# First tile's output and query projections as a three-pass float32r split, fed by six slots of whole weight rows

## The reference, cut to what matters

```python
h  = h + mixed @ w_out                        # (tokens, 2048) @ (2048, 2048), float32
x  = rmsnorm(h, norm2_g)
qq = x @ peer_wq                              # (tokens, 2048) @ (2048, 2048)
s1, s2 = per head: qq halves @ k1.T, qq halves @ k2.T
...                                           # top 16 of each, top 16 of their sums -> 128 experts a token
out = sum over the 128 experts e: g * gelu(x . U[e]) * V[e]
```

## Time and profile before

| | |
|---|---|
| median of 3 runs | 2587.0 us (2580.58 to 2588.91) |
| the profiled execution: its own time | 2590.78 us |
| the profiled execution: its span | 2588.2 us |
| TensorE matmul busy | 2221.9 us (86% of the span) |
| VectorE busy | 1452.6 us (56%) |
| ScalarE busy | 399.5 us (15%) |
| DMA | 845.85 MB, mean 327 GB/s |

### The profile page before, as it was taken

One profiled execution on the slowest core, in us unless ns is written; L12 is line 12 of the kernel. 1 busy time (PEld: TensorE's weight loads), 2 busy tenths in 40 slices (PEclk: granted clock), 3 DMA queues, 4 the chain that ended last, 5 costly groups with the idle time before them and its releaser, 6 DMA issues.

```text
span 2588.2 us, 20434 instructions
## 1 busy us (share of the span) xinstructions
PE 2221.9 (86%) x7522; PEld 1221.3 (47%) x7522; DVE 1452.6 (56%) x2649; ACT 399.5 (15%) x846; POOL 380.8 (15%) x363
## 2 busy tenths in 40 slices
PE   6999999887999899997999997777777877777776
PEld 6999999655654444443444443233232322222221
DVE  4433333677300366568544557887888855555554
ACT  4223222323101101002000011111111100000000
POOL 0000000001000111212122121222222221222221
PEclk9999999876999899999999999999999999999999
DMA  5544444312668999999999999999999999999997
GB/s 180 183 137 138 155 131 130 114 53 66 212 243 286 352 426 392 407 425 387 414 425 401 414 407 422 415 411 401 421 408 412 410 429 428 428 428 428 428 429 298
DMA packets 159899, 845.85 MB, mean 327 GB/s; under 512 B 9814, under 2 KB 97682, under 8 KB 117162
## 3 DMA queue, kind: packets, MB, share of 16 engines
q0 software_dynamic: 46080, 671.11, 61.6%
q1 hardware_dynamic: 113722, 173.45, 19.9%
HBM read 834.31 MB, written 10.21 MB: 326 GB/s over the span
## 4 chain that ended last, share of the span: by engine, by line
PE 55%; DMA 29%; DVE 10%; issue 4%; ACT 1%; SPq 0%; POOL 0%; DVEq 0%; POOLq 0%; ACTq 0%
DMA rows_in<-in_peer_uv,expert 28%; PE bank L250 20%; PE bank L276 8%; PE bank L1038 5%; PE bank L1039 5%; PE bank L1037 5%; PE bank L263 4%; DVE rows_in L552 3%; PE bank L1214 1%; PE bank L1204 1%; DVE diag L527 1%; PE bank L1022 1%; PE bank L1132 1%; PE bank L1191 1%; PE bank L1120 1%
## 5 line engine op out<-in xcount | busy, mean ns | idle before, releaser
L250 PE MATMUL bank<-rows_in,diag 128*128 128x512 f32 (+1 forms) x2560 | 1188.5, 612 | 269.2 <-DVE diag L527 268.9
L552 DVE CUSTOM_DVE_ANT_0 rows_in<-rows_in,x2n 128x2048 f32<-128x2048 f32 x320 | 733.6, 2292 | 529.1 <-DMA rows_in<-in_peer_uv,expert 528.9
L250 PEld LDWEIGHTS bank<-rows_in,diag 128*128 128x128 f32 (+1 forms) x2560 | 452.9, 183 | 986.4 <-issue 546.5
L458 POOL DMA_INDIRECT rows_in<-in_peer_uv,expert x320 | 365.8, 1143 | 1489.5 <-PE bank L250 1304.7
L360 ACT ACTIVATE dots<-dots 128x1 f32<-128x1 f32 x320 | 64.9, 203 | 1515.9 <-DVE dots L552 1515.9
L1037 PE MATMUL bank<-xnh,wh 128*128 128x336 f32 (+2 forms) x928 | 293.1, 316 | 4.7 <-DVE wl L1452 4.7
L1038 PE MATMUL bank<-xnl,wh 128*128 128x336 f32 (+2 forms) x928 | 291.4, 314 | 0.0
L1039 PE MATMUL bank<-xnh,wl 128*128 128x336 f32 (+2 forms) x928 | 291.2, 314 | 0.0
L1452 DVE TENSOR_TENSOR wl<-wring,wh 128x2048 fp32r<-128x2048 f32 (+1 forms) x58 | 132.1, 2279 | 230.0 <-ACT wh L1272 230.0
L1037 PEld LDWEIGHTS bank<-xnh,wh 128*128 128x128 f32 (+1 forms) x928 | 174.6, 188 | 6.7 <-issue 5.4
L1038 PEld LDWEIGHTS bank<-xnl,wh 128*128 128x128 f32 (+1 forms) x928 | 174.6, 188 | 1.3
(11 more groups left out here) (291 smaller groups left out, 1355.3 us busy)
## 6 DMA issues: line engine op xcount, KB each, us to landing
wring<-in_w_in SPq DMA_DIRECT2D x28, 2048.0 KB, 8.3
wk<-in_w_out SPq DMA_DIRECT2D x64, 512.0 KB, 7.9
wk<-in_peer_wq SPq DMA_DIRECT2D x64, 512.0 KB, 8.4
kT<-in_keys_t SPq DMA_DIRECT2D x16, 512.0 KB, 5.3
vpage<-in_cache_v SPq DMA_DIRECT2D x16, 512.0 KB, 4.9
rows_in<-in_peer_uv,expert POOLq DMA_INDIRECT x320, 12.5
C<-in_state_C SPq DMA_DIRECT2D x4, 1024.0 KB, 6.0
out_C_sample<-C SPq DMA_DIRECT2D x4, 1024.0 KB, 4.4
```

What stands on the lines that cost most here:

```text
L250: mm = pe.matmul(accs[t][d][0:w, :], diag[r % ND][:, 0:w], rows_in[r % NG][:, D + 512 * d:D + 512 * d + 512], start=False, stop=(j == ROUN ...
L458: nc.gpsimd.indirect_dma_start(out=rows_in[r % NG][:], out_offset=None, in_=UV_DR, in_offset=bass.IndirectOffsetOnAxis(ap=ids[:, j:j + 1], ...
L552: nc.vector.tensor_tensor_reduce(u, u, x2n[t][:], 1.0, 0.0, ALU.mult, ALU.add, dots[t % 2][:, j:j + 1]).then_inc(S["dot_done"], 1)
```

## The change

For tile 0 the products with `w_out` and `peer_wq` are done by the three-pass split. The stationary operand is kept as `lh` and `ll` (high and low; from `mixA`, and then from the transposed banks of the norm). Weights come as whole rows of 128 x 2048 floats (1 MB) into six slots `wf`; ScalarE writes the high part to one of four slots `wfh` (`weight_high`), VectorE writes the low part over the row itself (`wfl`, `weight_low`). A row is requested once the row six before it has been used. The tail of tiles 1 and 2 keeps its half rows, but its first six wait until tile 0's last whole row has been used, and so do `h1[1]`, `h1[2]` and `gf`, which stand ahead of them. The diff, with allocations of semaphores and removed lines of the old half-row order left out:

```diff
-NG, ND, NW = 4, 4, 6
+NG, ND, NW, NF, NH = 4, 4, 6, 6, 4
...
+    def full_read(eng, n):
+        part, k = n // KC, n % KC
+        if k == KC - 1:
+            take(eng, (("wo", "wq")[part], 0, 3))
+        else:
+            eng.wait_ge(S["wk_used"], (KC - 1) * part + k + 1)
     def tail_sync(sp, out):
...
+        def full_rows(w, part, rows_=range(KC)):
+            for k in rows_:
+                n = KC * part + k
+                if n >= NF:
+                    full_read(sp, n - NF)
+                sp.dma_start(wf[n % NF][:], w[P * k:P * k + P, :]).then_inc(wf_in[n % NF], 16)
+        def weight_rows(w, part):
+            for row in range(2 * KC):
+                r = 2 * KC * (part - 2) + row
+                k, f = row % KC, row // KC
+                if r < NW:
+                    full_read(sp, 2 * KC - 1)
...
         sp.wait_ge(S["iqz_done"], 1)
-        weight_rows(a["w_out"][0], 0, range(NW))
+        full_rows(a["w_out"][0], 0, range(3))
...
-        weight_rows(a["w_out"][0], 0, range(NW, KC))
         evacuated(sp, ("sT2",))
+        full_rows(a["w_out"][0], 0, range(3, KC // 2))
         sp.dma_start(h1[0][:], xp[0:P]).then_inc(S["xr_in"], 16)
-        weight_rows(a["w_out"][0], 0, range(KC, 2 * KC))
+        full_rows(a["w_out"][0], 0, range(KC // 2, KC))
         broadcast(g2, a["norm2_g"][0], "g2_in")
-        weight_rows(a["peer_wq"][0], 1, range(KC))
+        full_rows(a["peer_wq"][0], 1, range(KC // 2))
         sp.dma_start(kT12[:], a["keys"].rearrange("d (n k) -> d n k", n=2 * PH)).then_inc(S["keys_in"], 16)
-        weight_rows(a["peer_wq"][0], 1, range(KC, 2 * KC))
+        full_rows(a["peer_wq"][0], 1, range(KC // 2, KC))
+        take(sp, ("wq", 0, 3))
         sp.dma_start(h1[1][:], xp[P:2 * P]).then_inc(S["xr_in"], 16)
...
                 outs = [open_bank((key, 0, d)) for d in range(4)]
+                if part == 0:
+                    pe.wait_ge(S["lhs_lo"], 1)
                 for k in range(KC):
+                    n = KC * part + k
+                    pe.wait_ge(S["wk_lo"], n + 1)
                     for d in range(4):
-                        r = 2 * KC * part + 2 * k + d // 2
-                        pe.wait_ge(wk_in[r % NW], 16 * (r // NW + 1))
-                        mm = pe.matmul(outs[d][:], lhs[0][:, k, :], wk[r % NW][:, 512 * (d % 2):512 * (d % 2) + 512], start=(k == 0), stop=(k == KC - 1))
+                        cols = slice(512 * d, 512 * d + 512)
+                        pe.matmul(outs[d][:], lh[:, k, :], wfh[n % NH][:, cols], start=(k == 0), stop=False)
+                        pe.matmul(outs[d][:], ll[:, k, :], wfh[n % NH][:, cols], start=False, stop=False)
+                        mm = pe.matmul(outs[d][:], lh[:, k, :], wfl[n % NF][:, cols], start=False, stop=(k == KC - 1))
                         if k == KC - 1:
                             close(mm)
-                        elif d % 2:
-                            mm.then_inc(S["wk_used"], 1)
+                    if k < KC - 1:
+                        mm.then_inc(S["wk_used"], 1)
...
+    def weight_high(act, n):
+        act.wait_ge(wf_in[n % NF], 16 * (n // NF + 1))
+        if n >= NH:
+            full_read(act, n - NH)
+        nc.scalar.copy(wfh[n % NH][:], wf[n % NF][:]).then_inc(S["wk_hi"], 1)
+    def weight_low(dve, n):
+        dve.wait_ge(S["wk_hi"], n + 1)
+        nc.vector.tensor_tensor(wfl[n % NF][:], wf[n % NF][:], wfh[n % NH][:].bitcast(F32), ALU.subtract).then_inc(S["wk_lo"], 1)
     def tail_scalar(act, link):
...
             if g == 0:
+                for n in range(2, KC + 2):
+                    weight_high(act, n)
                 for d in range(4):
                     ins = squares_of(0, d)
...
-                    evacuate(("xt", t, q), x2T[t][:, 4 * q:4 * q + 4, :])
+                    if g:
+                        evacuate(("xt", t, q), x2T[t][:, 4 * q:4 * q + 4, :])
+                    else:
+                        b = take(act, ("xt", 0, q))
+                        nc.scalar.copy(lh[:, 4 * q:4 * q + 4, :], b[:].rearrange("p (n w) -> p n w", n=4)).then_inc(S["lhs_hi"], 1)
...
             if g == 0:
+                for n in range(KC + 2, 2 * KC):
+                    weight_high(act, n)
                 for d in range(4):
                     evacuate(("wq", 0, d), qqn[0][:, 512 * d:512 * d + 512])
...
+            if g == 0:
+                for n in range(2, KC + 2):
+                    weight_low(dve, n)
             dve.wait_ge(S["xr_in"], 64 if g else 16)
...
+            if g == 0:
+                for q in range(4):
+                    b = take(dve, ("xt", 0, q))
+                    dve.wait_ge(S["lhs_hi"], q + 2)
+                    give(nc.vector.tensor_tensor(ll[:, 4 * q:4 * q + 4, :], b[:].rearrange("p (n w) -> p n w", n=4),
+                                                 lh[:, 4 * q:4 * q + 4, :].bitcast(F32), ALU.subtract), ("xt", 0, q))
+                for n in range(KC + 2, 2 * KC):
+                    weight_low(dve, n)
...
             act.wait_ge(S["pz_zero"], 1)
+            act.wait_ge(S["m_sent"], 32)
+            nc.scalar.copy(lh[:], mixA[:]).then_inc(S["lhs_hi"], 1)
             for q in range(SB + 1):
...
+            for n in range(2):
+                weight_high(act, n)
             for n in range(2):
                 b = take(act, ("sO", n))
...
             for q in range(SB + 1):
+                if q == 2:
+                    dve.wait_ge(S["lhs_hi"], 1)
+                    nc.vector.tensor_tensor(ll[:], mixA[:], lh[:].bitcast(F32), ALU.subtract).then_inc(S["lhs_lo"], 1)
...
             give(ins, ("sQ",))
+            for n in range(2):
+                weight_low(dve, n)
             tail_vector(dve, link)
```

More of the change, by code:

```diff
@@ L185, in rounds_by @@
         return min(point, POINTS_B) * 3 // 2 + max(0, point - POINTS_B)
-    def tail_sync(sp, out):
[L189 to L205, removed]
+    def full_read(eng, n):
[4 more added lines that the diff above has]
+            eng.wait_ge(S["wk_used"], (KC - 1) * part + k + 1)
+    def tail_sync(sp, out):
+        def full_rows(w, part, rows_=range(KC)):
[11 more added lines that the diff above has]
+                else:
+                    last = r - NW
+                    if last % KC == KC - 1:
+                        take(sp, (("wo", "wq")[last // (2 * KC)], 2, 2 * (last // KC % 2) + 1))
+                    else:
+                        sp.wait_ge(S["wk_used"], 2 * (KC - 1) + last - last // KC + 1)
                 sp.dma_start(wk[r % NW][:], w[P * k:P * k + P, HD * f:HD * f + HD]).then_inc(wk_in[r % NW], 16)
@@ L271, in product @@
                 for k in range(KC):
-                    r = 2 * KC * part + KC * f + k
+                    r = 2 * KC * (part - 2) + KC * f + k
                     pe.wait_ge(wk_in[r % NW], 16 * (r // NW + 1))
@@ L287, in project @@
                 pe.wait_ge(S["mix_dup"], 1)
-            product(2 * g, (mixA,) if g == 0 else (mixB, mix2), beside)
+            product(2 * g, (mixB, mix2), beside)
             for _ in range(3):
@@ L771, in build @@
         wk = [at(f"wk{n}", 100352 + 4096 * n, [P, HD]) for n in range(NW)]
+        full_at = [100352 + 8192 * n for n in range(3)] + [62464 + 8192 * n for n in range(3)]
+        wf = [at(f"wf{n}", o_, [P, D]) for n, o_ in enumerate(full_at)]
+        wfl = [at(f"wfl{n}", o_, [P, D], FR) for n, o_ in enumerate(full_at)]
+        wfh = [at(f"wfh{n}", o_, [P, D], FR) for n, o_ in enumerate((46080, 54272, 29696, 37888))]
+        lh = at("lh", 16640, [P, KC, P], FR)
+        ll = at("ll", 176384, [P, KC, P], FR)
         TK = 124928
@@ L817, in build @@
             "qpad_zero", "qpad_done", "k_in0", "k_in1", "v_in0", "v_in1", "v_in2", "logitS_done", "expS_done", "probS_done",
-            "best_done", "gate_exp", "e_done", "wk_used", "xr_in", "g2_in", "keys_in", "norm_sq", "norm_ms", "norm_rms",
+            "best_done", "gate_exp", "e_done", "wk_used", "wk_hi", "wk_lo", "lhs_hi", "lhs_lo", "xr_in", "g2_in", "keys_in", "norm_sq", "norm_ms", "norm_rms",
             "x2n_done", "mix_dup", "c_rows",
@@ L824, in build @@
         wk_in = [sem(f"wk_in{n}") for n in range(NW)]
+        wf_in = [sem(f"wf_in{n}") for n in range(NF)]
         def take(eng, key):
```

## The result

The changed kernel takes 2566.21 us in the median of five runs (2561.73 to 2572.65), against 2588.91 us for the kernel before in the same session (2580.58 to 2594.32). The ratio is 0.9922 with a 95% interval of 0.990 to 0.9944: faster by 20 us, clear of the 0.3%, and 7 us under the forecast of 2573.4, only 0.7 us inside the fast end of its range. Two later comparisons of the same kernel gave 0.9953 (0.9922 to 0.9983) and 0.9931 (0.9909 to 0.9953); the three together say about 0.9935, 17 us. Single executions differ by far more: the kernel before ran from 2566.09 to 2595.11 us in one session. So a difference of a few us between two traces is not a difference between two kernels, and the first thing to do with the profiled execution of after (2561.73 us, span 2559.9) is not to believe its 28 us.

A forecast was written before the change was run, and what follows sets the result against it. The prediction took TensorE to bound tile 0's two products, with the gathers' DMA tail starting only behind them. The second product ending 14.8 us earlier, less 1.2, gave 13.6 off 2587.0: 2573.4 us, range 2565.5 to 2587.

The forecast's parts named there:

- TensorE's price: Tile 0's products: 0.227 us per float32r matmul of 512 columns, 2.72 us a row, 45.6 us a product with half clock.
- The first product: Tile 0's product with w_out: to end at 782.3 us, where it ended at 793.3.
- the channel's hold-up: Tile 0's first product: rows from 8 on, landing late, hold TensorE up by 0.7 us.
- The channel: Weight loads in tile 0: 401 GB/s, 2.61 us per 1 MB row; bounds 2.45 and 3.31 us.
- The first rival: Weight loads: channel gives less, 2.93 us a row; gain only 6.4 us, 2580.6 us; chance 0.18.
- the second, slower one: Weight loads: channel stays at 317 GB/s, 3.31 us a row; 3.9 us slower, 2590.9 us; chance 0.09.
- The norm behind row 17: Between tile 0's products: residual adds wait for row 17's conversion until 786.6 us; 4.3 us lost in waiting.
- The chain from the adds to the second product: Tile 0's norm, first add to second product: 11.9 us instead of 11.1, with the last ll subtraction new.
- Behind it: After tile 0's second product: late loads delay w_out's half row, covered by TensorE's slack; later gathers cost 1.2 us.
- the third rival: Tail of tiles 1 and 2: 3 MB of late loads take back 7.6 us; gain 7.2 us, 2579.8; chance 0.11.
- Sum: Whole kernel: second product ends 14.8 us earlier, less 1.2 behind it, 13.6 us gained.
- The fourth rival: Tile 0's products: float32r matmuls take two cycles a column; some 50 us slower, 2638 us; chance 0.04.

The follow-up runs named there:

- high_plain: The changed kernel with one plain float32 matmul of lh and wfh in place of the three float32r ones: ratio 1.000 to the kernel before.
- after2: The changed kernel once more, without an edit, for a second trace: ratio 0.9953 to the kernel before.
- after3: The changed kernel once more, without an edit, for a third trace: ratio 0.9931 to the kernel before.
- small_early: The changed kernel with h1[0] and g2 requested right behind the first three weight rows: ratio 0.9949 to the kernel before.
- best: The changed kernel with h1[0] and g2 requested early and row 17 converted behind the norm: ratio 0.9907 to the kernel before.
- before_xr_late: The kernel before, with h1[1], h1[2] and gf waiting until tile 0's second product is done: ratio 0.9999 to the kernel before.
- plain_whole: Whole rows in six slots as in the changed kernel, but plain float32 matmuls and no conversions: ratio 1.0024 to the kernel before.

## Why the prediction was right, and where it was off

- **TensorE's price.** 0.227 us a matmul from a cycle a column and 0.013: measured 0.227 (43.65 us for the 192 of a second product at full clock). 45.6 us for the second product: 45.1. high_plain shows that this step carries the gain.
- **The first product** was to end at 782.3: 783.0. It lasted 46.4 us, which is 43.5 and 2.9 of half clock (clock 0.78 in the first stretch, 736 to 750); the forecast had 2.1 for the half clock and 0.7 for the channel's hold-up (which add up to an end at 782.6, not 782.3). None of the hold-up is seen in the profiled execution, probably because the slow start let the loads get ahead. It is there in after2 and after3, which start at full clock: TensorE waits 1.12 and 1.09 us in the middle, for the row that stands behind `h1[0]` in the queue, and the product takes 45.9 and 45.7 us. The good fit of this term in one trace is partly luck. The end of the old product, 793.3 in the prediction, is 793.1 by its row.
- **The channel.** I took 2.61 us a row (401 GB/s); it was 2.49 (421 to 425), near the fast bound. The rule of the Trainium skill that I had weighed ("DMA: Bandwidth & Descriptors", "Where 436 GB/s comes from": about 358 GB/s from HBM) would have made it 2.93. This kernel's trace disagrees. The first rival and the second, slower one fall with it: their premise, that 317 GB/s at a share of 0.93 was near a ceiling, read a share as a limit (see the last section).
- **The norm behind row 17.** Forecast: adds at 786.6, 4.3 us behind the product. Measured: 785.92, 2.9 behind. The mechanism is shown by small_early and best, where the hold goes with the order of the loads and of the conversions. Row 17 came at 781.8, only 0.5 us before the forecast, though sixteen loads at 2.49 for 2.61 should give 1.9. Two rows came late: ScalarE has row 7 3.15 us behind row 6, and row 12 3.04 behind row 11. It isn't the half clock at the start: after2, at full clock, has row 12 3.77 us behind row 11, and row 17 as late, 45.3 us behind the product's start for 45.2. Why row 12 is late stays open.
- **The chain from the adds to the second product**: 11.9 forecast, 11.2 measured. Four full banks go faster than I had it: the squares start 0.61 us apart, not 0.63 + 0.19, because the accumulator's read (787.17 to 787.36) overlaps the next square (from 787.27).
- **Behind it.** The half row's landing was put at 11.2 us behind the product; TensorE got it at 13.7, a miss of 2.5 us. The wait was covered as said, so it cost nothing that the runs can tell. The 1.2 us that I took for later gathers lie within before_xr_late's interval of 5 us and are neither shown nor refuted; the third rival, the tail taking 7.6 us back, falls.
- **Sum.** The second product's end and the first gather: 14.8 us earlier forecast, 16.6 in the profiled execution; by tile 0's time 16.9, and 17.2 over three traces of each, of which the full clock in two of three traces of after, but one of three of before, is a part. Total: 13.6 forecast, 17 over the three comparisons. In the profiled execution the 1.8 us too little are the adds (0.7), the chain (0.7) and the second product (0.5). The tail's 1.2, taken off the forecast, is a term that no run shows. These were the mis-sized terms; the steps stood. The fits within each term are closer than the clock allows from one trace to the next, so the last us of them is luck.

The fourth rival, two cycles a column, is out by the same lines as TensorE's price.

## What to carry to other kernels

A float32 matmul of 512 columns was worth three float32r matmuls and 0.18 us more; that is only a gain if the two conversions and the loads stay under the new pace, so price a row on each engine and on the channel before, and keep the order of the smallest margins in mind (here 2.72 TensorE, 2.49 channel, 2.29 VectorE, 1.91 ScalarE). When one engine's work is done ahead in a loop, look at what stands behind the loop in the same queue: with two rows prepared for the next product the gap before it grew from 8.6 to over 14 us; asking for two other loads earlier gave about 4 of it back, and moving one conversion 1.3. Split a stretch into its parts, and look at the granted clock in each, before crediting an edit with a difference of one or two us. And take more than one trace of each kernel before explaining a difference of ten us in a part that the change doesn't touch.

## What I had not expected of the hardware

Loads had a different busy share for the same bytes. What seems to decide it is how much is outstanding, though no run varied that alone. With half rows the channel moved 317 GB/s at a share of 0.93; with whole rows wanted faster than they come, 425 at 1.02. It isn't the size of the request alone: in plain_whole all are 1 MB, and while it catches up after the start it moves 405 GB/s at 1.01, later, at TensorE's old pace, 307 at 0.87 and 161 at 0.46, that is about 350 for a full share:

```profile
740.00:755.00 15.00, 15.00 (x34) 6.55 (x34) 0.00 (x0) 0.00 (x0) 0.00 (x0) 0.94 1.01 405
755.00:770.00 15.00, 15.00 (x37) 6.63 (x36) 0.00 (x0) 0.00 (x0) 0.00 (x0) 1.00 0.87 307
...
830.00:856.00 26.00, 26.00 (x62) 11.59 (x61) 0.00 (x0) 0.00 (x0) 0.00 (x0) 1.00 0.46 161
```

So a share near 1 does not say that no more can be had. Nor are half rows slower as such: before moves 401 GB/s at 1.01 in 760 to 770, and 418 at 1.02 in 795 to 797, where the first product's end had let six half rows be requested.

TensorE's clock falls to its half (1.2 GHz) in the pause between the products, in every trace, but it comes back at a different time in each. after and after2 are one kernel, with a pause of 8.8 and 9.5 us and the same transposes behind it. In after the clock was 0.50 over 790 to 800, and the second product's first matmuls took 0.43 us instead of 0.227 until some 3 us in. In after2 the clock was back at 1.00 before the second product started:

```profile
789.05 0.47 PE L279 MATMUL bank<-wfh,lh 128*128 128x512 f32 x1 [1.67 <-DVE ll L642]
```

The same record took 0.77 us in after. Nine of the fourteen traces have the second product start at half clock, five at full; which it will be, nothing here tells.
